# Moving TensorE's moving operands from byte 32 to byte 96 of a 256-byte line in SBUF

## The reference

```
h = x
h += (b * conv(c*h')) @ w_out                 # b, c, h' = split(rms(h) @ w_in)
h += (silu(g) * u) @ w_down                   # g, u = split(conv(rms(h) @ w_up)), 1024 -> 5632 -> 1024
h += attention(rms(h)) @ w_o                  # 8 heads, latent q (512), k and v (256)
h += (silu(g) * u) @ w_down                   # the same shape again
h = rms(h)
h += mod2 * (rms(o) * silu(r)) @ w_o          # gated linear attention, 4 heads, context and latent, both directions
h += mod5 * relu(rms(h) @ w1)**2 @ w2         # 1024 -> 4096 -> 1024
return rms(h)
```

## Time and profile before

| | |
|---|---|
| median of 3 runs | 940.62 us |
| the profiled execution | 940.77 us, of which its span is 939.0 us |
| PE, matmuls | 927.7 us busy (99%), 6944 instructions |
| DVE | 797.8 us busy (85%) |
| ACT | 563.4 us busy (60%) |

### The profile page before, as it was taken

One profiled execution on the slowest core, in us unless ns is written; L12 is line 12 of the kernel. 1 busy time (PEld: TensorE's weight loads), 2 busy tenths in 40 slices (PEclk: granted clock), 3 DMA queues, 4 the chain that ended last, 5 costly groups with the idle time before them and its releaser, 6 DMA issues.

```text
span 939.0 us, 19746 instructions
## 1 busy us (share of the span) xinstructions
PE 927.7 (99%) x6944; PEld 883.9 (94%) x6944; DVE 797.8 (85%) x1333; ACT 563.4 (60%) x932; POOL 1.8 (0%) x8
## 2 busy tenths in 40 slices
PE   9999999999999999999999999999999999999997
PEld 8999999999999899999999998988899988888886
DVE  6999899999989889899999997865868989886553
ACT  6645666666455666666666556976533667774432
POOL 0000000000000000000000000000000000000000
PEclk9999999999999999999999999999999999999998
DMA  8777576558776555565557865564774457777561
GB/s 306 239 265 234 184 276 203 187 183 279 251 270 208 170 183 161 178 201 187 193 181 268 275 236 186 179 220 130 233 247 155 130 157 261 239 232 217 191 189 45
DMA packets 53877, 195.55 MB, mean 208 GB/s; under 512 B 6110, under 2 KB 6366, under 8 KB 53696
## 3 DMA queue, kind: packets, MB, share of 16 engines
q1 hardware_dynamic: 53680, 193.78, 62.5%
q10 hardware_dynamic: 144, 1.05, 0.3%
HBM read 193.76 MB, written 1.05 MB: 207 GB/s over the span
## 4 chain that ended last, share of the span: by engine, by line
PE 92%; DVE 5%; ACT 1%; issue 1%; DVEq 0%; ACTq 0%
PE ps L503 24%; PE ps L499 19%; PE ps L500 19%; PE ps L502 10%; PE ps L531 2%; PE ps L533 2%; PE ps L532 2%; DVE wlo L1525 2%; PE ps L610 1%; PE ps L791 1%; PE ps L807 1%; PE ps L652 1%; PE ps L654 0%; PE ps L653 0%; PE ps L677 0%
## 5 line engine op out<-in xcount | busy, mean ns | idle before, releaser
L1525 DVE TENSOR_TENSOR wlo<-raw,whi 128x1024 fp32r<-128x1024 f32 x303 | 366.7, 1220 | 71.6 <-ACT whi L1006 70.9
L1006 ACT ACTIVATE whi<-raw 128x1024 fp32r<-128x1024 f32 x303 | 316.9, 1052 | 87.7 <-PE ps L503 53.2
L503 PE MATMUL ps<-x,wlo 128*128 128x256 f32 x1248 | 349.0, 280 | 0.0
L499 PE MATMUL ps<-x,whi 128*128 128x256 f32 x1024 | 288.1, 281 | 0.0
L500 PE MATMUL ps<-x,whi 128*128 128x256 f32 x1024 | 285.9, 279 | 0.0
L503 PEld LDWEIGHTS ps<-x,wlo 128*128 128x128 f32 x1248 | 235.2, 188 | 0.0
L499 PEld LDWEIGHTS ps<-x,whi 128*128 128x128 f32 x1024 | 192.8, 188 | 0.8 <-issue 0.5
L500 PEld LDWEIGHTS ps<-x,whi 128*128 128x128 f32 x1024 | 192.8, 188 | 0.6 <-issue 0.5
L500 PE MATMUL ps<-ylo,whi 128*128 128x256 f32 x400 | 111.7, 279 | 0.0
L499 PE MATMUL ps<-yhi,whi 128*128 128x256 f32 x400 | 111.7, 279 | 0.0
L503 PE MATMUL ps<-yhi,wlo 128*128 128x256 f32 x400 | 111.7, 279 | 0.0
(11 more groups left out here) (329 smaller groups left out, 1532.4 us busy)
## 6 DMA issues: line engine op xcount, KB each, us to landing
raw<-stream SPq DMA_DIRECT2D x343, 512.0 KB, 4.0
side<-stream SPq DMA_DIRECT2D x16, 512.0 KB, 4.7
h<-xT SPq DMA_DIRECT2D x2, 512.0 KB, 5.8
c<-ctxT ACTq DMA_DIRECT2D x1, 1024.0 KB, 7.5
out<-h SPq DMA_DIRECT2D x4, 256.0 KB, 2.5
ct<-cst SPq DMA_DIRECT2D x1, 898.5 KB
rt_tab<-rot SPq DMA_DIRECT2D x1, 768.0 KB
state<-crow SPq DMA_DIRECT2D x1, 512.0 KB, 6.8
```

The source lines that it names most:

```text
L499: pe.matmul(dst, whi[:, w], at(hi, k), start=(k == 0), stop=False)
L503: last = pe.matmul(dst, wlo[:, w], at(hi, k), start=False, stop=(k == K - 1))
L1006: c.sig(act.activation(whi[:, s * D:(s + 1) * D], raw[:, r * D:(r + 1) * D], ACT.Copy), hi_ready)
L1525: c.sig(dve.tensor_tensor(wlo[:, w], raw[:, r], whi[:, w], ALU.subtract), slots_done)
```

## The change

`line_pad` grows from 32 to 48 elements, 64 bytes more, so that everything behind it starts 64 bytes later. A new tensor `z_pad` of 48 elements (192 bytes) stands ahead of `zhi` and `zlo`, which so start 256 bytes later and at the same place within a 256-byte line as before. Nobody reads or writes the pads. On all five engines the instructions, their order, their shapes and their waits are the same in both kernels; only addresses differ.

```diff
@@ -206,7 +206,7 @@
         ee = sb("ee", 4 * GH)
         state = sb("state", 2 * GH * T)
 
-        sb("line_pad", 32)
+        sb("line_pad", 48)
         stage = ExitStack()
         x2 = sb("x2", 2 * DC * T, F32R, stage)
         xhi, xlo = x2[:, 0:DC * T], x2[:, DC * T:2 * DC * T]
@@ -262,6 +262,7 @@
         rt_tab = sb("rt_tab", NROT, F32, stage)
         c32 = sb("c32", DC * T, F32, stage)
         rstd_c = sb("rstd_c", T, F32, stage)
+        sb("z_pad", 48, F32, stage)
         zhi = sb("zhi", DC * T, F32R, stage)
         zlo = sb("zlo", DC * T, F32R, stage)
         stage.close()
```

## The result

The changed kernel takes 956.72 us (median of 4 runs, 956.43 to 957.14), the kernel before 940.29 us beside it. The ratio is 1.0174, with a 95% interval from 1.0162 to 1.0186: 16.4 us slower. 956 had been forecast.

The account below looks back on a forecast made before the run. PE's own work, 92% of the chain of waits, was taken as the bound. 5440 x 2.5 ns = 13.6 us and 448 x 3.3 ns = 1.5 us add 15.1 us to 940.62, giving 956 us, range 947 to 963.

Parts of the forecast that it names:

- What bounds the kernel: Whole kernel: PE's own work is 92% of the chain of waits, so time is matmul count times pitch plus seams.
- the 24 cycles over one per column: 256-column matmuls from byte 32: 280 cycles each, the excess put down to PE's operand fetching, not other engines' traffic.
- Reading the pitch by place: Matmul pitch compared by the moving operand's start byte: 116.7 ns at byte 32, 118.8 ns at byte 128.
- The price of one matmul: Added cost of a 256-column matmul moved from byte 32 to 96: 2.5 ns, within -3.3 to 3.3 ns.
- The raw 3.3 ns of the upper end: Upper bound on a matmul's added cost, from the stretch with `ulo` at byte 96: 120.0 - 116.7 ns.
- The 2.1 ns of `z`: Extra pitch where `zhi` and `zlo` move from byte 128, against byte 32; used in choosing 2.5 ns.
- The count: Matmuls with 256 columns whose moving operand goes from byte 32 to 96: 5440, at 2.5 ns, 13.6 us.
- the second term: The 448 matmuls with 512 columns in two runs, at 3.3 ns each: 1.5 us.
- What costs nothing: Weight loads, `z` and `u` matmuls, fp32 matmuls, DVE, ACT and `side` transfers: taken as no added time.
- No change, by the place within 64 bytes: Rival: only the start within 64 bytes counts, so 32 and 96 are the same: 940.6 us, chance 0.25.
- Faster, by fewer collisions further apart: Rival: moving operand's reads collide with weight loads, less so 96 bytes apart: 925.5 us, chance 0.18.
- The stretch at 117.9 ns that I couldn't place: 42 matmuls on `x2` at byte 32, from 606.56 to 611.51 us, 1.2 ns slower for an unknown reason.

Follow-up runs that it names:

- e1: Against the kernel before, weights moved from byte 0 to 64 and activations from 32 to 96, distance still 32: 940.27 us, ratio 0.9999.
- e10: Against the kernel before, weights moved from byte 0 to 64, activations left at byte 32, distance -32: 950.13 us (one run).
- e11: Against the kernel before, `zhi` and `zlo` moved from distance 128 to 32 and `ulo` from 96 to 32: 940.28 us, ratio 0.9997.
- e9: Against the kernel before, `wlo` starts at byte 64 and activations at 96, `whi` stays at byte 0: 954.90 us (one run).
- e2: Against the kernel before, activations moved from byte 32 to 160, weights left at byte 0: 943.93 us, ratio 1.0034.
- e5: Against the kernel before, activations moved 256 bytes further on, to distance 288, weights at byte 0: 940.67 us (one run).
- e8: Against the kernel before, `x2` alone moved to distance 96, the tiles behind it left at byte 32: 952.15 us, ratio 1.0120.

## Why the prediction was right, point by point

- *What bounds the kernel.* Right, and it carries everything: PE's busy time rose by 17.1 us and the span by 16.4. That the pitch doesn't go by DMA's or DVE's traffic is borne out by the last projection, 120.0 ns with DMA at nothing. Where the 24 cycles over one per column come from, no run shows: the edits added up to 8 to them and never took one away.
- *Reading the pitch by place.* Right as a warning: every other place in the trace of before was slower than byte 32, and so was byte 96. Wrong as a reason: I read the place of the moving operand, and e1 and e10 show that it is the distance to the weights. In the kernel before the weights are at byte 0, so the two can't be told apart from its trace. It was luck that this reading served: the change moved the activations alone. Had it moved the weights with them, as e1 does, the same reasoning would have forecast a loss where there is none.
- *The price of one matmul.* Mis-sized: 2.5 ns taken, 3.2 measured (119.9 - 116.7). The raw 3.3 ns of the upper end was closer. That the earlier trace rows came so close is partly chance. In e11, with `ulo` alone moved to distance 32, the pitch of the triples there fell from 120.0 to 119.1 ns; if prices simply added, which e9 contradicts, `ulo` at 96 had cost some 2.7 ns and its neighbours `uhi` the rest. The 2.1 ns of `z` belong to distance 128, and a look at 48 or 64 would have given 1.6 or 1.1.
- *The count.* 5440 took in the 448 L503 that stand behind an L502. These don't pay: a whole pair went from 346.7 to 350.0 ns, which the second term already held (its 3.3 ns came from comparing two different shapes, so that it fits is luck). With the measured prices, 4992 x 3.2 = 16.0 and 448 x 3.3 = 1.5 make 17.5 us, near the 17.1 us of PE's busy time. The high count (448 x 2.5 = 1.1 us) made up for a third of the low price (4992 x 0.7 = 3.5 us), and 0.7 us came back from PE's idle time: 15.1 forecast, 16.4 measured.
- *What costs nothing.* Right: `z` kept 137 in 16 us, DVE's means moved by 1 ns at most, `side` lands in the same 4.7 us. The fp32 matmuls cost nothing either, but in most of them (`kn` with `qn`, `att` with `gv`) both operands moved together and the distance stayed, so they don't test the price. The 96 matmuls in which `x2` is stationary and 512 columns of weights move were not in the sum at all; by the starts in the trace they went from 233.2 to 234.1 ns, 0.1 us.
- *No change, by the place within 64 bytes.* Refuted by the result (32 and 96 differ by 64 bytes), and e2 against e5 leaves a period of 256 bytes. By the Trainium skill, "SBUF — State Buffer", section "Door 1: The DMA port swizzle", lines of 16 bytes are what matters for full bandwidth. The trace doesn't agree that this is all: distances 0, 16, 32, 48, 64 and 96 are all multiples of 16, and cost 119.9, 118.5, 116.7, 118.3, 117.8 and 119.9 ns.
- *Faster, by fewer collisions further apart.* That the two streams of reads meet is the part that the runs favour: it takes both places to tell the pitch. That they collide, and where, no run shows. The sign was wrong: 96 bytes apart is slower, and 32 is the best of the eight distances tried for 256 columns.
- *The stretch at 117.9 ns that I couldn't place*. e2 and e8 show that one distance has more than one steady pitch. What picks one stays open; no run was made on it. In e2 and e8 the pitch changes between stages and then holds through a whole stage.

## What to carry to other kernels

Where TensorE is full and each 256-column fp32r matmul carries its own weight load, the start of the moving operand less that of the weights, by its remainder to 256 bytes, was worth up to 3.2 ns a matmul, 1.7% of this kernel, with no instruction changed. So after any edit to a layout compare the pitch of the matmuls (their count in a full stretch) and not only busy shares: one matmul more or less in 114 us is 0.1 ns, and in a stretch without idle time a change of it isn't a wait. Move weights and activations together or neither.

## What the runs showed of the hardware that I had not expected

- The pitch depends on the distance of two operands, not on either one's place: 940.27 us at (64, 96) and 940.29 at (0, 32), 956.72 at (0, 96) and 950.13 at (64, 32), weights first.
- The curve has a narrow best place: 118.5 ns at 16, 116.7 at 32, 118.3 at 48, 117.8 at 64, 119.9 at 96. That 48 is worse than 64 rests on one execution each.
- Each shape has its own best distance. 512 moving columns in one run are fastest where 256 are slowest: 228.3 ns at distance 0, against 233.3 at -32. A pair of 512 columns in two runs and 256 takes 346.7 ns at 32 and at 160, and 360.0 at 16.
- The same loop on the same operands can run at 118.7 or 117.3 ns a matmul (e2), without idle time and at the same clock; the mixer of the same execution runs at 119.9.
- Two distances in one chain don't average: 116.7 ns with `z` 128 bytes from `whi` and 64 from `wlo` (e9), against 118.7 with 128 from both and 117.8 with 64 from both.
